# Token ranks dealt over slot groups, and the first two weight blocks split by token halves, in a hybrid SSD and mixture-of-experts step

## The reference

```python
t = rmsnorm(x)                                  # 592 x 1024
g_sel = argmax(softmax(t @ w_rg + b_rg))        # one of 4 expert groups
top_v, top_i = top_k(softmax(le[g_sel]), 2)     # two of its 8 experts
gate = one_hot(g_sel) * one_hot(top_i) * top_v / sum(top_v) * g_prob
for g in range(4):
    a, up = t @ w_gate[g], t @ w_up[g]          # per expert 1024 x 256
    out += (silu(a) * up * gate[g]) @ w_down[g] # per expert 256 x 1024
```

## Time and profile before

| | us |
|---|---|
| median of 3 runs | 1330.32 |
| lowest, highest | 1326.76, 1331.12 |
| the profiled execution | 1328.34 |
| its span on the core | 1326.5 |
| TensorE busy | 1202.8 (91%) |
| VectorE, ScalarE, GpSimd busy | 532.5, 386.8, 459.0 |
| granted TensorE clock, mean | 0.965 of 2.4 GHz |

### The profile page before, as it was taken

The page is one execution under the profiler, slowest core; times in us unless marked ns, Lnnn a source line. Parts: engine busy times, 40 slices in busy tenths (PEclk is TensorE's granted clock), DMA queues, the critical chain, the costliest instruction groups (busy, mean ns, idle before and its releaser), DMA issues.

```text
span 1326.5 us, 22266 instructions
## 1 busy us (share of the span) xinstructions
PE 1202.8 (91%) x8729; PEld 1031.4 (78%) x8729; DVE 532.5 (40%) x839; ACT 386.8 (29%) x568; POOL 459.0 (35%) x358
## 2 busy tenths in 40 slices
PE   4999999999999999999999999999997988787781
PEld 4999999999976986997798599999995654344340
DVE  5345442003655765675485651123433241111112
ACT  4111114433424433342443361122324100010012
POOL 5344432333533454363454434344320112111200
PEclk7999999999999999999999999999997989989996
DMA  6233322232412610621352032443649999999975
GB/s 155 65 79 79 79 80 64 64 86 79 125 46 71 160 48 16 182 81 33 104 131 60 25 112 80 101 127 93 222 162 351 398 399 405 402 397 380 398 256 157
DMA packets 185563, 210.62 MB, mean 159 GB/s; under 512 B 12166, under 2 KB 161798, under 8 KB 176754
## 3 DMA queue, kind: packets, MB, share of 16 engines
q1 hardware_dynamic: 176626, 193.41, 44.0%
q0 software_dynamic: 5040, 9.72, 3.0%
q10 hardware_dynamic: 3822, 6.39, 1.3%
HBM read 191.56 MB, written 26.57 MB: 164 GB/s over the span
## 4 chain that ended last, share of the span: by engine, by line
PE 73%; DMA 10%; DVE 6%; SPq 6%; issue 3%; ACT 2%; DVEq 0%; ACTq 0%; POOLq 0%
PE acc L641 48%; SPq L562 6%; PE acc L914 4%; PE pTS L1025 4%; DMA area<-in_w_up 2%; DMA area<-in_w_gate 2%; DMA ring<-in_w_gate 2%; DMA ring<-in_w_up 2%; DVE area L1229 2%; PE pTS L814 2%; PE acc L1066 1%; PE pY L808 1%; PE pY L832 1%; PE acc L773 1%; PE pO L762 1%
## 5 line engine op out<-in xcount | busy, mean ns | idle before, releaser
L641 PE MATMUL acc<-h_parts,ring_parts 128*128 128x328 f32 (+1 forms) x3840 | 545.9, 303 | 11.0 <-DVE h_parts L1122 6.9
L641 PEld LDWEIGHTS acc<-h_parts,ring_parts 128*128 128x128 f32 x3840 | 532.2, 190 | 25.7 <-issue 20.1
L1888 POOL TENSOR_TENSOR ring_parts<-ring,ring_parts 128x1024 fp32r<-128x1024 f32 x112 | 280.8, 2507 | 436.4 <-ACT ring_parts L1596 436.3
L1596 ACT ACTIVATE ring_parts<-ring 128x1024 fp32r<-128x1024 f32 x112 | 118.5, 1058 | 396.0 <-PE acc L641 370.1
L1025 PE MATMUL pTS<-area,big 128*64 128x256 f32 x672 | 109.6, 408 | 16.3 <-DMA area<-in_w_gate 6.7
L641 PE MATMUL acc<-u_parts,ring_parts 128*128 128x264 f32 (+1 forms) x640 | 109.4, 299 | 0.0
L1025 PEld LDWEIGHTS pTS<-area,big 128*64 128x64 f32 x672 | 66.6, 147 | 51.9 <-issue 10.8
L641 PEld LDWEIGHTS acc<-u_parts,ring_parts 128*128 128x128 f32 x640 | 96.4, 188 | 0.0
L641 PE MATMUL acc<-area_parts,ring_parts 128*128 128x264 f32 (+1 forms) x512 | 91.1, 299 | 0.0
L1229 DVE SCALAR_TENSOR_TENSOR area<-area,xvec 128x616 f32<-128x616 f32 x72 | 84.9, 1179 | 10.5 <-DVE area L1227 0.6
L641 PEld LDWEIGHTS acc<-area_parts,ring_parts 128*128 128x128 f32 x512 | 78.4, 188 | 0.0
(11 more groups left out here) (353 smaller groups left out, 1440.1 us busy)
## 6 DMA issues: line engine op xcount, KB each, us to landing
ring<-in_w_in SPq DMA_DIRECT2D x80, 512.0 KB, 4.0
area<-in_w_gate SPq DMA_DIRECT2D x21, 1024.0 KB, 24.5
area<-in_w_up SPq DMA_DIRECT2D x21, 1024.0 KB, 24.9
area<-in_w_down SPq DMA_DIRECT2D x21, 1024.0 KB, 24.7
area<-in_state_ssm SPq DMA_DIRECT2D x16, 512.0 KB, 7.0
out<-area SPq DMA_DIRECT2D x16, 512.0 KB, 5.3
ring<-in_w_ssd_out SPq DMA_DIRECT2D x16, 512.0 KB, 3.7
ring<-in_w_gate SPq DMA_DIRECT2D x7, 1024.0 KB, 24.6
```

The source lines that it names most:

```text
L641: m = nc.tensor.matmul(acc[a][:, h, 0:n], w[s][:, k, :], x[:, k, h * HALF:h * HALF + n], start=first and k == 0 and w is w_hi and x is hi, ...
L1596: a_.activation(w_hi[b % 2], w_raw[b % 2], ACT.Copy).then_inc(hi_done, 1)
L1888: gp.tensor_tensor(w_lo[b % 2], w_raw[b % 2], w_hi[b % 2].bitcast(F32), ALU.subtract).then_inc(lo_done, 1)
```

## The change

It has two parts. In the first, the first turn of the first loop is written out: blocks 0 and 1 run half 0 of each, then half 1 of each; half 0 waits for token tiles 0 to 2, half 1 for all. VectorE's three tiles are counted by a semaphore of their own, `h_rest`, so `h_lo` counts two tiles and later a third event. In the second, `places` holds another order: slot 4a + b holds rank a + 16b, so that ranks 0 to 15 lie in slots 0, 4, 8 ... 60, ranks 16 to 31 in slots 1, 5, 9 ... 61, and so on.

```diff
-        s_un = sem("s_un")
+        s_un, h_rest = sem("s_un"), sem("h_rest")
...
-            pe.wait_ge(h_lo, TILES)
-            with pe.Fori(0, 4) as t:
+            pe.wait_ge(h_lo, 2)
+            for part in range(2):
+                pe.wait_ge(h_rest, 1 if part == 0 else TILES - 2)
+                for b in range(2):
+                    pe_block(pe, s_block(0, b), b, hT_hi, hT_lo, part=part)
+            for b in range(2, 6):
+                pe_block(pe, s_block(0, b), b, hT_hi, hT_lo)
+            with pe.Fori(1, 4) as t:
                 for b in range(6):
                     pe_block(pe, s_block(t, b), b, hT_hi, hT_lo)
...
-                    pe.wait_ge(h_lo, TILES + 1)
+                    pe.wait_ge(h_lo, 3)
...
             for i in range(2, TILES):
                 dve.wait_ge(h_hi, i + 1)
                 v.tensor_tensor(hT_lo[:, :, tok(i)], hT[:, :, tok(i)], hT_hi[:, :, tok(i)].bitcast(F32), ALU.subtract
-                                ).then_inc(h_lo, 1)
+                                ).then_inc(h_rest, 1)
...
-            gp.iota(places, pattern=[[1, CAP]], base=0, channel_multiplier=0, allow_small_or_imprecise_dtypes=True)
+            gp.iota(places.rearrange("p (a b) -> p a b", b=4), pattern=[[1, CAP // 4], [CAP // 4, 4]], base=0, channel_multiplier=0, allow_small_or_imprecise_dtypes=True)
```

## The result

| kernel | median us | lowest to highest | ratio to before |
|---|---|---|---|
| before | 1328.61 (5 runs) | 1326.76 to 1331.12 | |
| changed | 1317.45 (5 runs) | 1313.47 to 1318.06 | 0.991 (95% interval 0.9891 to 0.9928) |

The change is worth 11.2 us. The profiled execution of the changed kernel took 1317.78 us, with a span of 1316.0, 10.5 under the span before.

What follows compares the result with a forecast made beforehand. TensorE bounds projections and scan to about 985 us, weight transfers the expert stage. From 1328.34, minus 4.3 (start), 7.8 (levelling) and 0.3 (last scatter), gives 1315.9, predicted as 1316; range 1308 to 1323.

Steps and rivals of the forecast that it cites:

- The first matmul: Start of block 0 on TensorE: to begin at about 22.9 us and not 27.4, 4.5 us earlier.
- The stall at block 2: TensorE waiting for block 2's weight split, covered only by block 1's second half: 0.2 us, between 0 and 0.6.
- The clock at the start: TensorE's rise to 2.4 GHz: 5.8 us after starting keeps 4.5 us; fixed at 33.2 leaves 2.2; sooner adds 0.9.
- The start's term: Gain from halving the first two blocks: 4.3 us, with ends 2.0 and 5.2.
- The same shift still there at 985 us: Sign for the halved start: its gain of some 4 us persists to the end of projections and scan.
- The levelling: Expert stage: dealt ranks even out the DMA engines' rows, so weights end 7.8 us sooner, between 5.8 and 9.7.
- The last scatter: Final scatter, alone on the engines: one row fewer in a full group saves 0.3 us, between 0 and 1.5.
- landing times below 24.5 us: Sign for the dealt ranks: expert weight loads land in under 24.5 us.
- (a): Rival: only the start pays, the expert stage being limited by a rate all engines share; 1324 us; 0.14 together with (c).
- (b): Rival: engines hold slots 16 or 4 apart, so dealing heaps full places on a quarter of them; 1353 us; chance 0.04.
- (c): Rival: block 2's stall and a low clock cost 2.5 us, levelling at its lower end or half; 1323; 0.14 with (a).
- (d): Rival: start, levelling and last scatter all at their upper ends; 1311.9 us, inside the forecast's own range.

Runs made afterwards that it cites:

- order A0, A1, B0, B1: Changed kernel with both token halves of block 0 run before both halves of block 1; 1313.70 us, ratio 0.9887.
- halves alone: Kernel before with the halved first two blocks and the old order of the ranks; 1322.83 us, ratio 0.9955.
- dealt ranks alone: Kernel before with only the new slot order of the ranks, without the halved blocks; 1320.60 us, ratio 0.9931.
- changed kernel's second trace: Profiled execution of the unchanged repeat of the changed kernel in a later session; that repeat measured 1315.04 us, ratio 0.9913.
- kernel without addition: Scatters write rows instead of adding them, against the changed kernel with block 0's halves run before block 1's; 1304.26 us, ratio 0.9825.
- the heap: Kernel before with ranks 0 to 3 in slots 0 to 3, ranks 4 to 7 in slots 32 to 35, and so on; 1340.77 us, ratio 1.0085.
- two finer orders: Block 0's halves before block 1's, ranks dealt back and forth over eight pairs of slot groups, 1313.50 us; that with partner groups exchanged, 1311.82 us.
- finest order: Kernel with ranks dealt back and forth, plus partner expert groups exchanged in the second eight pairs; 1311.82 us, ratio 0.9881.

## Why the prediction was right, point by point

**The total.** 1316 was forecast with 1308 to 1323; 1317.45 and 1315.04 were measured. The sum was 12.4 us for the profiled execution, the spans differ by 10.5.

**The first matmul** was put at 22.9 us and came at 22.45: VectorE's subtraction began 0.15 us sooner, and the gap behind it is 0.1 us and not the 0.35 taken from the old wait. 4.9 us in place of 4.5.

**The stall at block 2** was 0.2, between 0 and 0.6; it is 0.37, and the wait names GpSimd's split, as the step said. The order A0, A1, B0, B1 takes it away.

**The clock at the start.** The three cases were: rise 5.8 us after the first matmul, rise at a fixed time, or sooner. The mean from 20 to 30 us is 0.59 in the first trace, so it rose at 30 - 10 x 0.18 = 28.2, 5.8 us after the first matmul; in the halves alone 0.66 gives 26.8, 4.9 us after its first matmul at 21.9. So the gain of the first matmul was kept whole, in the second case with 0.45 us more: the rise came 0.9 us sooner, and a microsecond at the low clock costs half of one. The start's term was 4.3 with an upper end of 5.2; 5.5 to 5.6 stands at the transposes where the clock falls as often as before, and 6.0 (4.0 to 8.0) in time. It was a little too small.

**"The same shift still there at 985 us"** failed in the first trace: 1.5 of 5.0. The step said that nothing lies between; it left out that the clock falls for a few microseconds at times while TensorE is busy. The dealt ranks alone show the same falls, and the changed kernel's second trace is without the second. The kernel without addition, which has the halved start and the dealt ranks, is without the first. The second belongs to the execution; the first follows neither part of the change.

**The levelling** was 7.8, between 5.8 and 9.7; 8.3 and 8.4 in the stage with both parts, 7.1 alone. The mechanism is shown, and that the size fits is partly luck. The 9.7 was called the gain of perfect levelling, as if the old order cost time in the staircase alone. It doesn't: the stage gained 8.3 us and 3.8 us of the staircase are still unused, so more than 9.7 was there to gain. What the prediction put at nothing, without a reason, is the 243 us ahead of the staircase, where the engines move 401 GB/s and not 397; at the same bytes that is 2.4 us (1.8 to 3.0 with the rounding). The staircase itself gave 9.7 - 3.8 = 5.9, which is the prediction's lower end, and 5.9 + 2.4 = 8.3. The middle of the two ends hit because it had too much for the one part and nothing for the other. In the heap the staircase is no worse than before and the rate makes the whole loss.
The rows' price of 0.54 us for both ways, times the 21 rows that the Trainium skill's assignment moves, gave 11.3 and was too much; for the 23 rows of the heap it gave 12.4, and 11.0 were measured. The assignment fits, and the price per row was too high by a third for the dealt order, by a tenth for the heap.

**The last scatter**: 0.3 forecast, 0.45 measured in the first trace. The spread is as large: it took 5.77 and 5.51 us in the two traces of the changed kernel, 5.90 with the dealt ranks alone, 6.22 and 6.60 in the two kernels with the old order. The heap's took 5.96, less than the old order's, which the fullest engine doesn't explain.

**Marks named ahead.** The last gate load was to land 12 us sooner and landed 9.8 (13.9 in the second trace, at 1274.3). The staircase was to fall from 1 to 0 in under 10 us. That isn't decided: it goes from 0.94 at 1271 to 0.25 at 1280, ten windows, and the next scatter cuts it off. One mark was wrong: landing times below 24.5 us. For the changed kernel the page gives

```profile
area<-in_w_gate SPq DMA_DIRECT2D x21, 1024.0 KB, 25.4
...
area<-in_w_down SPq DMA_DIRECT2D x21, 1024.0 KB, 23.7
```

and 24.5 and 24.7 before. The one rose and the other fell. SyncE issues a load as soon as its place is free, so a faster stage may only fill the queue sooner; this is a reading and no run isolates it. TensorE's waits for weights did not grow: 37.0 us in seven rows from 1010 to 1283 us, where 44.0 stood before. It was not late next.

**The rivals.** (a) the shared rate fell with the dealt ranks alone and with the heap. (b) the opposite assignment fell with the dealt ranks alone, which are faster and not slower, and with the heap. (c) and (d) were sizes, 1323 and 1311.9, and both measured times lie between them.

**What stays open.** Why the order of the slots changes the rate ahead of the staircase, at a DMA share of 1.02 before and after. Why the price per row falls as the engines come level: 0.48 us a row in the heap (11.0 / 23), 0.40 in the dealt order (8.3 / 21; 0.34 where it stands alone, 7.1 / 21), 0.1 to 0.2 in the two finer orders (0.4 / 4, or 0.8 / 4 against the changed kernel, and 1.0 / 6). That the mean of the engines begins to count as the fullest comes near it fits the unused part, which is down to 1.1 us in the finest order, and no run isolates it. Why dealing alone left 5.5 us unused and 3.8 together with the halves isn't known, nor what makes the clock fall while TensorE is busy.

## What to carry to other kernels

When a stage is bound by DMA, look at its last 20 microseconds in windows of one: if the share falls in a staircase, the engines carry unequal loads. Its length less the area under it is what levelling can give at that place, here 9.7 us, and no upper bound for the whole: the dealt order took 5.9 us of it and 2.4 more from the rate ahead of it, and the heap lost 11 us with a staircase no worse than before. So compare the rate of the long stretch too. Indirect transfers with unused slots can be a source of this, since packed indices leave the same slots empty each time; spread them over the partitions. And when a block can start on half of its input, run both of its halves before the next block's, unless the second half's input is still late: the next split is then covered by a whole block. Here that was 0.45 us in the trace and too little to see in the time.

## What the runs showed of the hardware

- Which slots the rows lie in shifts a whole kernel: 1320.6, 1329.6 and 1340.8 us for three orders of 64 slots with the same rows and bytes, at 401, 397 and 380 GB/s over 243 us of weight loads.
- An adding scatter costs the DMA engines more than a writing one: some 0.18 us of an engine more for a row of 4 KB (3.0% and 2.0% of 16 engines' span), 5.93 against 3.62 us for the last scatter alone, 10.4 us over the stage with 18 of them, and 1582 against 1009 ns of GpSimd's time to issue one.
- The granted clock falls to 1.2 GHz for a few microseconds with TensorE busy all through, in some executions and not in others: from 215 to 235 us the mean clock is 1.00 in the trace of before and in the one without addition, and 0.91 in the others, from 295 to 315 us it is 0.91 before, 0.83 and 1.00 in the changed kernel, 0.86 with the dealt ranks alone, with TensorE busy 20.00 of 20 us in each. The changed kernel's first trace has 6.8 us more at 1.2 GHz there than the trace of before, which is 3.4 us of its gain, more than the interval's half width (2.5).
